# Modulation sums of a transformer kernel: VectorE turns the rows in 32 by 32 blocks, four products with stacked identities add the quarters

## The chip, the cores and the metric

The kernel runs on one core of a Trainium2 chip. A core has TensorE (PE, with its weight loads as PEld), VectorE (DVE), ScalarE (ACT), GpSimd (POOL) and SyncE (SP, which issues transfers), on-chip memory SBUF with 128 partitions, and PSUM, eight banks that TensorE writes. The metric is the device time of one execution in microseconds (us).

## The reference, cut to what matters

The program runs two blocks on 256 tokens of width 1024. The first has two layers of a gated feed-forward part, a mixing part (Fourier mixing, dilated attention, differential attention, gates) and a second feed-forward part. The second block has one layer of attention and a mixture of 32 experts, modulated by a vector `c`:

```python
c_act = jax.nn.silu(c)                                   # (1, 1024)
mod = (c_act @ w_ada[l] + b_ada[l])[:, None, :]          # 6 x 1024 values
shift1, scale1, gate1, shift2, scale2, gate2 = jnp.split(mod, 6, axis=-1)
h = _rmsnorm(x, norm1_w[l]) * (1.0 + scale1) + shift1
```

The modulation is a product of one row with a matrix of 1024 x 6144. It depends on no other result, so the kernel computes it earlier, inside the first block.

## The kernel before, in words

Activations lie transposed in SBUF: 128 channels of a group on the partitions, 256 tokens along. Weights come as a stream of tiles of 1.5 MB into a ring of four, mostly three units of 128x1024 to a tile. ScalarE rounds each unit to its high part (`round_unit`, L467), VectorE takes the rest as its low part (`low_unit`, L864), and TensorE multiplies with three products for each block (L1413, L1416, L1417, and L1444 to L1448 in `project_tok`). Four buffers of each part let the engines run ahead of TensorE.

The two layers of the first block are one loop (`Fori(0, LAYERS)`). Each engine has its own program with its own fixed order, tied to the others by semaphores. In a layer the steps are: feed-forward, projections, attention in 12 steps u (four dilated, eight differential), the V20 projection (eight units, c = 0 to 7), the Fourier mixing, gates and branches, output, feed-forward.

The modulation tiles lie in the stream: seven (`ADA_TILES`) in each layer, two behind the loop. `ada_tile` (L1481) multiplies one of them on TensorE in attention step u, from u = 6 on. Its weight operand `cpad` is 32 columns wide, of which only the first holds silu(c). Each of the four groups of 32 PSUM partitions gets two of the eight channel groups, so the sum of a modulation value lies in four quarters, in partitions 0, 32, 64 and 96 of bank 5, in 384 columns; the other rows are zero. ScalarE copies these 128x384 values to SBUF (`ada_sb`, L608; L656 behind the loop), as its last work of the step, and raises `ada_row`, for which TensorE waits before the next tile. `ada_sums` (L1490) then makes columns of the rows: for each tile and each 128 of its 384 values one product, whose weight is the 128x128 block of `ada_sb` and whose moving operand is one column of ones:

```python
for i in range(n):
    pe.wait_ge(ada_row, rows + i + 1)
    for j in range(ADA_COLS):
        at = 384 + i * ADA_COLS + j
        mm = mm_(ps[:, bank, at:at + 1], ada_sb[i][:, j * P:(j + 1) * P], ones[:, 0:1], start=True, stop=True)
```

These are 21 products in each layer, behind unit c = 2 of V20 (L1602), and 6 behind the loop, behind the first unit of the second block (L1687). The products are in fp32, and each is two records in the trace. VectorE copies the resulting columns to `mod` at c = 3 (L1039).

In an attention step VectorE scales the logits and adds the bias (`scores`, L1003, then the maximum at L1008 or L1010), and then divides the exponentials of the step before (`probs`, L1017 to L1022). TensorE does the logits of u (L1550), the transposes of u - 2 (L1559), the values of u - 3 (L1568, L1579) and then the modulation tile (L1487). ScalarE does the exponentials (L580, L584), copies the transposes (L590), the outputs (L605) and the modulation rows (L608).

Of the kernel before, what the change touches and what calls it, by code (L numbers as in the profile page):

```python
# [11 lines left out]
ALU = mybir.AluOpType  # L12
ACT = mybir.ActivationFunctionType
# [96 lines left out]
def build(nc, stream, experts, x_in, konst_in, cpad_in, layer_in, lam_in, cols_in, relb_in, onehot_in, konst1_in,  # L110
          konst2_in, bias_rows, out):
    with ExitStack() as ctx:
# [32 lines left out]
        lamv = rest("lamv", 18432, LAYERS, 4 * DH)  # L145
# [20 lines left out]
        ada_sb = [rest(f"ada_sb{i}", 16384 + 384 * i if i < 5 else 3328 + 384 * (i - 5), 384) for i in range(ADA_TILES)]  # L166
# [93 lines left out]
        rel_landed, konst1_landed, konst2_landed = sem("rel_landed"), sem("konst1_landed"), sem("konst2_landed")  # L260
        cpad_ready, cols_landed = sem("cpad_ready"), sem("cols_landed")
# [195 lines left out]
        def _(a):  # L457
# [83 lines left out]
            with a.Fori(0, LAYERS) as l:  # L541
# [51 lines left out]
                for u in range(UNITS + 3):  # L593
# [12 lines left out]
                    if 6 <= u < 6 + ADA_TILES:  # L606
                        a.wait_ge(ada_used, l * ADA_TILES + (u - 5))
                        nc.scalar.activation(ada_sb[u - 6][:, :], ps[:, 5, 0:384], ACT.Copy).then_inc(ada_row, 1)  # L608
# [45 lines left out]
            for i in range(2):  # L654
                a.wait_ge(ada_used, L * ADA_TILES + i + 1)
                nc.scalar.activation(ada_sb[i][:, :], ps[:, (3, 0)[i], 0:384], ACT.Copy).then_inc(ada_row, 1)  # L656
# [199 lines left out]
        def _(v):  # L856
# [85 lines left out]

            for i in range(OUTS):
                v.wait_ge(xt_ready, i + 1)
                nc.vector.tensor_copy(x[:, 2 * i:2 * i + 2, :], ps[:, 4 + i, :].rearrange("p (a b) -> p a b", b=TOK)).then_inc(x_ready, 1)
            v.wait_ge(par_landed, 16)
# [5 lines left out]
            with v.Fori(0, LAYERS) as l:  # L952
# [73 lines left out]
                for u in range(UNITS + 1):  # L1026
                    if u < UNITS:
                        scores(u)
                    if 1 <= u <= UNITS:
                        probs(u - 1)  # L1030
                    if u == 7:
                        v.wait_ge(ob_hi, l + 1)
                        nc.vector.tensor_tensor(obs[:, 1, :], ps[:, 6, 0:TOK], obs[:, 0, :].bitcast(F32), ALU.subtract).then_inc(ob_taken, 1)
                low_unit(l, V20 + 2)
# [56 lines left out]
            v.wait_ge(cols_landed, 16)  # L1091
            recip_std(Q)
# [308 lines left out]
        def _(pe):  # L1401
# [88 lines left out]
            def ada_sums(n, bank, rows):  # L1490

                for i in range(n):
                    pe.wait_ge(ada_row, rows + i + 1)
                    for j in range(ADA_COLS):
                        at = 384 + i * ADA_COLS + j
# [698 lines left out]
```

## Time and profile before

| | |
|---|---|
| median of 3 runs | 2830.42 us (2827.72 to 2830.92) |
| profiled execution | 2826.78 us, span 2825.0 us |
| granted TensorE clock, mean | 0.966 of 2.4 GHz |
| PE busy | 2669.5 us (94%), 19672 matmul records |
| DVE busy | 1435.2 us (51%) |
| ACT busy | 942.2 us (33%) |
| DMA, mean over the span | 251 GB/s |

Rows of the profile give start and duration in microseconds, the engine, the line of the kernel and the operation with the names and shapes it writes and reads. `128*32 128x384` on a matmul is a weight of 128 rows and 32 columns and 384 moving columns. A bracket `[1.43 <-PE ps L1550]` says how long the engine sat idle before and what ended it. Repeated rows are merged as `xN`, with the time from the first to the end of the last.

### The profile page before, as it was taken

The page shows a single profiled execution, that of the slowest core. Times are in us where ns is not written, and L with a number is a line of the kernel's source. Part 1 is how long each engine was busy: PE and PEld are TensorE (multiplying, and loading weights), DVE is VectorE, ACT ScalarE, POOL GpSimd, SP SyncE. Part 2 cuts the span into 40 slices and gives each one's busy share as a digit, 9 for nine tenths or more (in the row PEclk, how much of TensorE's full clock was granted, in tenths as well). Part 3 has the DMA queues.
Part 4 walks back from the last instruction along what each step waited for, and adds up shares of the span by engine and source line. Part 5 has one row for each costly group of instructions (what it writes and reads, how often), then busy time and mean ns, then how long its engine had stood idle before and what let it go on. Part 6 is the DMA issues. An engine that isn't in the chain of part 4 may idle for free.

```text
span 2825.0 us, 49664 instructions
## 1 busy us (share of the span) xinstructions
PE 2669.5 (94%) x19672; PEld 2150.2 (76%) x19673; DVE 1435.2 (51%) x2586; ACT 942.2 (33%) x1471; POOL 30.5 (1%) x21
## 2 busy tenths in 40 slices
PE   7999999999899999999979879799999999999996
PEld 6999689999899868999968869755555555555553
DVE  5665556666566555666656775423333333333333
ACT  4444444443444445444434534211111111111111
POOL 0000000000000000000000210000000000000000
PEclk8999999999999989999989989889999999999997
DMA  8644535455355453445433324469999999999994
GB/s 257 235 178 158 223 113 184 161 187 183 140 187 186 158 238 131 179 157 179 182 152 135 112 90 148 158 268 430 429 431 429 431 430 430 430 430 430 430 430 201
DMA packets 70406, 709.15 MB, mean 251 GB/s; under 512 B 10983, under 2 KB 11239, under 8 KB 13303
## 3 DMA queue, kind: packets, MB, share of 16 engines
q1 hardware_dynamic: 65144, 699.30, 61.8%
q0 software_dynamic: 5152, 8.31, 1.4%
q8 instruction: 77, 1.26, 0.2%
q14 instruction: 33, 0.27, 0.0%
HBM read 703.89 MB, written 3.67 MB: 250 GB/s over the span
## 4 chain that ended last, share of the span: by engine, by line
PE 70%; DMA 19%; DVE 7%; ACT 2%; issue 2%; SPq 0%; DVEq 0%; ACTq 0%
DMA slot<-in_experts 19%; PE ps L1413 15%; PE ps L1416 15%; PE ps L1417 15%; PE ps L1898 5%; PE ps L1881 4%; PE ps L1923 3%; PE ps L1936 1%; PE ps L1408 1%; PE ps L1444 1%; PE ps L1447 1%; PE ps L1448 1%; DVE u_lo L864 1%; PE ps L1487 1%; PE ps L1550 1%
## 5 line engine op out<-in xcount | busy, mean ns | idle before, releaser
L864 DVE TENSOR_TENSOR u_lo<-ring,u_hi 128x1024 fp32r<-128x1024 f32 x500 | 615.8, 1237 | 498.9 <-ACT u_hi L467 495.2
L467 ACT ACTIVATE u_hi<-ring 128x1024 fp32r<-128x1024 f32 x498 | 523.7, 1057 | 705.2 <-PE ps L1413 633.1
L1413 PE MATMUL ps<-hs,u_hi 128*128 128x256 f32 x2408 | 692.3, 287 | 24.4 <-DVE hs L883 22.9
L1416 PE MATMUL ps<-hs,u_hi 128*128 128x256 f32 x2408 | 685.7, 285 | 0.0
L1417 PE MATMUL ps<-hs,u_lo 128*128 128x256 f32 x2408 | 685.6, 285 | 0.0
L1413 PEld LDWEIGHTS ps<-hs,u_hi 128*128 128x128 f32 x2408 | 466.6, 194 | 36.2 <-DVE hs L883 22.8
L1898 PE MATMUL ps<-slot,xg 128*64 128x256 f32 x4096 | 472.0, 381 | 10.1 <-DMA slot<-in_experts 9.7
L1416 PEld LDWEIGHTS ps<-hs,u_hi 128*128 128x128 f32 x2408 | 466.7, 194 | 0.5
L1417 PEld LDWEIGHTS ps<-hs,u_lo 128*128 128x128 f32 x2408 | 466.6, 194 | 0.0
L1898 PEld LDWEIGHTS ps<-slot,xg 128*64 128x64 f32 x4096 | 290.9, 137 | 222.9 <-issue 74.1
L1923 PE MATMUL ps<-slot,eact 128*64 128x512 f32 x1024 | 249.2, 607 | 5.6 <-DMA slot<-in_experts 5.1
L1344 DVE TENSOR_SCALAR lin<-ps,konst 128x64 f32<-128x64 f32 x256 | 71.3, 278 | 333.2 <-PE ps L1908 333.2
L1335 DVE SCALAR_TENSOR_TENSOR y_tok<-ps,wt,y_tok 128x512 f32<-128x512 f32 x128 | 90.2, 747 | 248.8 <-PE ps L1936 248.8
L1413 PE MATMUL ps<-acts,u_hi 128*128 128x256 f32 x704 | 199.7, 284 | 3.4 <-DVE acts L911 3.4
L803 ACT ACTIVATE hid_tok<-ps 128x256 f32<-128x256 f32 x128 | 49.0, 383 | 457.5 <-PE ps L1898 457.5
L1416 PE MATMUL ps<-acts,u_hi 128*128 128x256 f32 x704 | 199.2, 283 | 0.0
L1417 PE MATMUL ps<-acts,u_lo 128*128 128x256 f32 x704 | 199.2, 283 | 0.0
L1881 PEld LDWEIGHTS ps<-place,h_tok 128*128 128x128 f32 x1024 | 120.0, 196 | 27.4 <-issue 23.1
L1923 PEld LDWEIGHTS ps<-slot,eact 128*64 128x64 f32 x1024 | 62.1, 136 | 101.5 <-issue 97.3
L1413 PEld LDWEIGHTS ps<-acts,u_hi 128*128 128x128 f32 x704 | 135.1, 192 | 4.2 <-issue 4.2
L1416 PEld LDWEIGHTS ps<-acts,u_hi 128*128 128x128 f32 x704 | 135.1, 192 | 0.0
L1417 PEld LDWEIGHTS ps<-acts,u_lo 128*128 128x128 f32 x704 | 135.1, 192 | 0.0
(313 smaller groups left out, 3077.8 us busy)
## 6 DMA issues: line engine op xcount, KB each, us to landing
slot<-in_experts SPq DMA_DIRECT2D x256, 1536.0 KB, 20.4
ring<-in_stream SPq DMA_DIRECT2D x184, 1536.0 KB, 6.4
slot<-in_experts SPq DMA_DIRECT2D x4, 1024.0 KB, 4.8
bias<-bias_rows POOLq DMA_DIRECT2D x2, 1280.0 KB, 11.3
konst<-in_konst POOLq DMA_DIRECT2D x1, 2272.0 KB, 14.7
bias_rows<-vecs POOLq DMA_DIRECT2D x3, 512.0 KB, 14.1
x_tok<-in_x SPq DMA_DIRECT2D x1, 1024.0 KB, 5.3
bias_rows<-vecs POOLq DMA_DIRECT2D x1, 1024.0 KB, 70.6
```

Source lines behind the costliest of these rows:

```text
L467: nc.scalar.activation(u_hi[buffer_of(l, k)][:, :], raw_unit(l, k), ACT.Copy).then_inc(unit_hi, 1)
L803: nc.scalar.activation(hid_tok[:, j % 2, :], ps[:, j % 2, 0:2 * P], ACT.Copy).then_inc(htok_copied, 1)
L864: nc.vector.tensor_tensor(u_lo[b][:, :], raw_unit(l, kk), u_hi[b][:, :].bitcast(F32), ALU.subtract).then_inc(unit_lo, 1)
L1335: nc.vector.scalar_tensor_tensor(out=ys, in0=ps[:, 6 + half, :], scalar=wt[:, t, bass.ds(e, 1)], in1=ys, op0=ALU.mult, op1=ALU.add).then_i ...
L1344: nc.vector.tensor_scalar(lin[:, j % 2, h, :], ps[:, 3, h * P + CAP:h * P + 2 * CAP], konst2[:, bass.ds(e * 16 + (K2_BEXP + DC + c), 1)], ...
L1408: mm = mm_(ps[:, SSUM, 0:TOK], ones, sq[:, c, :], start=c == 0, stop=c == DC - 1)
L1413: mm = mm_(dst, hi, x_hi, start=first, stop=False, skip_group_check=True)
L1416: mm_(dst, hi, x_lo, start=False, stop=False, skip_group_check=True)
L1417: return mm_(dst, lo, x_hi, start=False, stop=last, skip_group_check=True)
L1881: mm = mm_(ps[:, 2, c * CAP:(c + 1) * CAP], h_tok[:, t, c * P:(c + 1) * P], place[:, t, 0:CAP], start=t == 0, stop=t == TT - 1)
L1898: mm = mm_(ps[h * CAP:(h + 1) * CAP, j % 2, 0:2 * P], xg[:, b, k * PAIRS + c, :], slot(2 * j + k)[:, at:at + 2 * P], start=k == 0 and c == ...
L1923: mm = mm_(ps[h * CAP:(h + 1) * CAP, 4, :], eact[:, j % 2, k, :], slot(sl)[:, at:at + 512], start=j == 0 and k == 0, stop=j == PAIRS - 1 a ...
```

## The change

VectorE takes over from ScalarE. Instead of a copy it does a `transpose` of the 128x384 PSUM values into `adaT`, which turns each block of 32x32 by itself: the value in partition 32q, column 32b + i comes to partition 32q + i, column 32b. `turn_ada` waits for the tile (`ada_used`) and stands before `scores(u)` for u = 7 to 11, before the last `probs` at u = 12, and once more behind the steps; the two behind the loop stand before the first `recip_std`. The weight of the sums is now `quarters`, four stacked 32x32 identities, made once at the start of the program by a `tensor_reduce` over the identity. Four products, one for each group r of 32 output partitions, take every 128th column of `adaT` from 32r on and so add the four quarters of all n tiles at once (21 moving columns in a layer, 6 behind the loop). `lamv` moves to another place in SBUF, `adaT` lies at 16384, where most of `ada_sb` was.

```diff
-        lamv = rest("lamv", 18432, LAYERS, 4 * DH)
+        lamv = rest("lamv", 3328, LAYERS, 4 * DH)
...
-        ada_sb = [rest(f"ada_sb{i}", 16384 + 384 * i if i < 5 else 3328 + 384 * (i - 5), 384) for i in range(ADA_TILES)]
+        adaT = rest("adaT", 16384, ADA_TILES * 384)
+        quarters = rest("quarters", 19072, 32)
...
-                    if 6 <= u < 6 + ADA_TILES:
-                        a.wait_ge(ada_used, l * ADA_TILES + (u - 5))
-                        nc.scalar.activation(ada_sb[u - 6][:, :], ps[:, 5, 0:384], ACT.Copy).then_inc(ada_row, 1)
...
-            for i in range(2):
-                a.wait_ge(ada_used, L * ADA_TILES + i + 1)
-                nc.scalar.activation(ada_sb[i][:, :], ps[:, (3, 0)[i], 0:384], ACT.Copy).then_inc(ada_row, 1)
...
+            def turn_ada(l, i, bank):
+
+                v.wait_ge(ada_used, l * ADA_TILES + i + 1)
+                nc.vector.transpose(adaT[:, i * 384:(i + 1) * 384], ps[:, bank, 0:384]).then_inc(ada_row, 1)
...
+            v.wait_ge(konst_landed, 16)
+            nc.vector.tensor_reduce(quarters[:, :], ident.rearrange("p (a b) -> p b a", b=32), AX.X, ALU.add).then_inc(quarters_ready, 1)
...
                 for u in range(UNITS + 1):
+                    if 7 <= u <= UNITS:
+                        turn_ada(l, u - 7, 5)
                     if u < UNITS:
                         scores(u)
...
+                turn_ada(l, ADA_TILES - 1, 5)
                 low_unit(l, V20 + 2)
...
+            for i in range(2):
+                turn_ada(L, i, (3, 0)[i])
             recip_std(Q)
...
-                for i in range(n):
-                    pe.wait_ge(ada_row, rows + i + 1)
-                    for j in range(ADA_COLS):
-                        at = 384 + i * ADA_COLS + j
-                        mm = mm_(ps[:, bank, at:at + 1], ada_sb[i][:, j * P:(j + 1) * P], ones[:, 0:1], start=True, stop=True)
+                pe.wait_ge(ada_row, rows + n)
+                for r in range(4):
+                    mm = mm_(ps[32 * r:32 * r + 32, bank, 384:384 + n * ADA_COLS], quarters[:, :], adaT[:, 32 * r:n * 384:P], start=True, stop=True)
                 mm.then_inc(ada_cols, 1)
...
             pe.wait_ge(vec_taken, 4)
+            pe.wait_ge(quarters_ready, 1)
```

## Rows read from the trace of the kernel before

**Rows 1.** The page, part 4: the chain that ended last, by engine.

```profile
PE 70%; DMA 19%; DVE 7%; ACT 2%; issue 2%; SPq 0%; DVEq 0%; ACTq 0%
```

**Rows 2.** The chain of waits, layer 1: start us, us, what.

```profile
343.91 5.52 PE ps L1496 x42
349.44 0.64 PE ps L1444
...
354.12 0.30 PE ps L1444
```

**Rows 3.** The chain of waits, layer 2.

```profile
1045.89 4.58 PE ps L1496 x42
1050.47 0.51 PE ps L1444
...
1054.59 0.23 PE ps L1444
...
1057.02 0.23 PE ps L1444
```

**Rows 4.** By stretches: us, PE, PEld, DVE, ACT, POOL busy, clock, DMA share, GB/s.

```profile
343.90:349.40 5.50, 5.50 (x44) 5.50 (x42) 0.16 (x1) 0.00 (x0) 0.00 (x0) 0.81 0.89 371
349.40:354.10 4.70, 4.70 (x14) 4.12 (x14) 1.32 (x2) 1.06 (x1) 0.00 (x0) 0.50 0.04 14
354.10:361.70 7.60, 7.60 (x39) 6.77 (x38) 3.68 (x3) 3.19 (x3) 0.00 (x0) 1.00 0.50 171
...
1050.40:1054.10 3.70, 3.70 (x12) 3.12 (x12) 1.31 (x2) 1.06 (x1) 0.00 (x0) 0.54 1.04 442
```

**Rows 5.** The timeline of TensorE behind the loop: start us, us, what.

```profile
1450.82 1.39 PE L1496 MATMUL ps<-konst,ada_sb 128*128 128x1 f32 x12
1452.07 0.47 PE L1444 MATMUL ps<-u_hi,hs 128*128 128x512 f32 x1
```

**Rows 6.** The timeline of TensorE's weight loads at a modulation tile.

```profile
1420.52 0.13 PEld L1487 LDWEIGHTS ps<-ring,cpad 128*32 128x32 f32 x4 [0.19 <-issue]
```

**Rows 7.** The timeline of VectorE (and one weight load) in the attention steps, layer 1.

```profile
320.30 0.42 DVE L1033 TENSOR_TENSOR obs<-ps,obs 128x256 fp32r<-128x256 f32 x1
320.81 0.69 DVE L1003 SCALAR_TENSOR_TENSOR S<-ps,bias 128x512 f32<-128x512 f32 x1
...
322.77 0.48 DVE L1022 SCALAR_TENSOR_TENSOR S<-S,small 128x256 f32<-128x256 f32 x1
...
329.76 0.69 DVE L1003 SCALAR_TENSOR_TENSOR S<-ps,bias 128x512 f32<-128x512 f32 x1 [0.59 <-PE ps L1550]
...
332.33 0.17 DVE L1020 RECIPROCAL small<-small 128x2 f32<-128x2 f32 x1
...
332.99 0.48 DVE L1022 SCALAR_TENSOR_TENSOR S<-S,small 128x256 f32<-128x256 f32 x1
...
334.92 0.20 PEld L1559 LDWEIGHTS ps<-konst,S 128*128 128x128 f32 x2 [0.62 <-issue]
...
339.09 1.23 DVE L864 TENSOR_TENSOR u_lo<-ring,u_hi 128x1024 fp32r<-128x1024 f32 x1 [5.61 <-ACT u_hi L467]
```

**Rows 8.** Single lines of VectorE: durations in ns (min/median/max); one timeline row.

```profile
L945 DVE COPY x<-ps x4: 680/692/692, 7.7 to 10.0; 128x512 f32<-128x512 f32 x4
...
303.30 0.96 DVE L1003 SCALAR_TENSOR_TENSOR S<-ps,bias 128x768 f32<-128x768 f32 x1 [1.60 <-PE ps L1550]
...
L1018 DVE TENSOR_SCALAR S<-S,small x8: 619/620/622, 298.5 to 1011.2; 128x768 f32<-128x768 f32 x8
...
L1042 DVE RECIPROCAL std<-std x2: 6553/6553/6553, 367.4 to 1067.8; 128x1024 f32<-128x1024 f32 x2
```

**Rows 9.** The timelines of ScalarE and VectorE in V20, layer 2.

```profile
1047.35 1.06 ACT L467 ACTIVATE u_hi<-ring 128x1024 fp32r<-128x1024 f32 x1 [4.14 <-DMA ring<-in_stream]
...
1048.43 1.22 DVE L864 TENSOR_TENSOR u_lo<-ring,u_hi 128x1024 fp32r<-128x1024 f32 x1 [3.60 <-ACT u_hi L467]
```

**Rows 10.** By stretches, in the dilated steps of layer 1.

```profile
297.00:301.00 4.00, 2.00 (x9) 1.40 (x9) 3.90 (x7) 1.64 (x4) 0.00 (x0) 0.82 0.00 0
301.00:305.00 4.00, 4.00 (x14) 2.74 (x13) 2.33 (x4) 1.72 (x3) 0.00 (x0) 0.50 0.00 0
```

More of the change, by code:

```diff
@@ L260, in build @@
         rel_landed, konst1_landed, konst2_landed = sem("rel_landed"), sem("konst1_landed"), sem("konst2_landed")
+        quarters_ready = sem("quarters_ready")
         cpad_ready, cols_landed = sem("cpad_ready"), sem("cols_landed")
```

## The prediction

> **What bounds the kernel now.** I read the page first, then the chain of waits around the lines that the change touches, then the timeline of each engine there, then the clock by stretches. TensorE carries 70% of the chain that ended last, VectorE 7% and ScalarE 2% [rows 1]. So what leaves TensorE's queue should shorten the program unless another engine takes its place.
>
> In the chain of layer 1 the reader sees the sums at L1496: 42 records, 5.52 us in one piece, with no other engine in between [rows 2]. Behind them the next unit starts at 349.44 and the one after it at 354.12: 4.68 us for a unit of products that takes 2.43 us undisturbed (1054.59 to 1057.02) [rows 3]. The stretches explain it: the granted clock is 0.81 during the sums, 0.50 (1.2 GHz of 2.4) for the 4.7 us behind them, and 1.00 again after that [rows 4]. The engine had work all the time, but work of one column each, and the clock fell. Layer 2 shows the same: 4.58 us of sums, then a unit that takes 4.12 us from 1050.47 to 1054.59 [rows 3], at a clock of 0.54 [rows 4]. The third place, behind the loop, has only 12 records: 1.25 us from the first to the product behind them, which is not a slow one [rows 5].
>
> **The change part by part.**
>
> *Sums removed.* Layer 1: 5.52 us of records, and 4.68 - 2.43 = 2.25 us lost by the clock, with 0.07 in the product at 354.12 (0.30 for 0.23): 2.3. Layer 2: 4.58, and 4.12 - 2.43 = 1.7. Third place: 1.25. Together 5.52 + 2.3 + 4.58 + 1.7 + 1.25 = 15.4 us, all in TensorE's queue and on the chain.
>
> *Four products in their place.* Each fp32 product is two records (21 products are 42), so there are 8 records, three times. No row shows a 32-column weight with 21 columns moving. Nearest are those of the modulation tiles: 32-column weights, four column groups side by side, four loads in 0.13 us with 0.19 us of issue before them, so 0.32 us for four [rows 6]; 8 records make 0.64. From below: loads alone, 0.26 us. From above: the pace of the old records, 4.58/42 = 0.109, makes 0.87, with 0.3 us more for the change of weight shape before and after: 1.2. I take 0.7 us, as the modulation rows are the nearest: 2.1 us for three. That a stretch of 8 records lets the clock stay up is read from the third place, where 12 did [rows 5].
>
> Balance of TensorE: 15.4 - 2.1 = 13.3 us.
>
> *Turning in place of ScalarE's copies.* ScalarE loses 16 copies of 0.48 us. In every step it waits for VectorE's maxima, so this is worth nothing. VectorE gains 16 turns of 128x384 from PSUM. The trace has no such operation. A copy of 128x512 from PSUM takes 0.69 us, and the scores (L1003) grow from 0.69 at 512 columns to 0.96 at 768, 1.05 ns a column [rows 7, 8], so a copy of 384 columns would take 0.69 - 0.13 = 0.56 us. From below: the 768 columns of L1018 in 0.62 us are 0.81 ns a column all told, 0.31 us. From above: VectorE's slowest row, the reciprocal, 6.4 ns a column [rows 8], 2.46 us. I take 0.56 us, for it reads the same memory with one input and no arithmetic.
>
> The Trainium skill speaks against this value. "VectorE: DVE Perf Modes", section "The three transpose paths", gives 311 ns for a 128x128 block turn in bf16, and three such are an estimate of 0.93 us; the microarchitecture page ("Vector Engine (DVE) Microarchitecture Reference", section 3.8) has the turn sustain one element per cycle and lane, which is near the 0.56 us. No row here decides between them; by 0.93 us the sum would be 3 us smaller.
>
> *What a turn costs in the attention steps.* There is one step per modulation tile, and VectorE is nearly as full as TensorE. From the start of the scores (L1003) to the end of the last probabilities (L1022) are 323.25 - 320.81 = 2.44 us; then it waits some 0.6 us for the next logits [rows 7]. The turn stands before the scores. The first, at u = 7, fits into VectorE's wait for that step's logits and costs nothing. The second follows L1033, which ends at 320.72, where there is no idle time: with 0.56 and 0.02 of handing over, the scores start at 321.32, not at 320.81. From there a step of VectorE takes 2.44 + 0.58 = 3.02 us against the 2.98 of now (320.81 to 329.76 in three), so three steps later the last scores start at 321.32 + 9.06 = 330.38 instead of 329.76: 0.62 us late. Queued behind the waiting turn are the scores and probabilities of the step; for the probabilities wait TensorE's transposes. The turn at u = 12 stands before the last probabilities: 330.38 + 2.44 + 0.58 + 1.14 (L1020 to L1022) = 334.54, some 0.5 us to hand over, and TensorE comes to the last transposes only at 334.92 [rows 7] + 0.62, behind its last tile, so nothing is added. Cost: 0.6 us a layer, 1.2 in all. The seventh turn lies in the 5.61 us idle before 339.09 [rows 7], the two behind the loop where VectorE waits for the root.
>
> *The wait on the turns moved.* TensorE's wait before a tile is met when the turn ends, about when the scores start; its tile comes behind transposes and values of the same step. The sums' wait is long met by c = 2. The reduction that makes the stacked identities and TensorE's wait for it stand where VectorE idles for the first unit: nothing. So is the place of lamv.
>
> *What comes late next.* With the sums gone TensorE needs later units sooner. In layer 1 none waits for a transfer. In layer 2 ScalarE waited 4.14 us for the tile of unit 93 (c = 5), and VectorE made its low part by 1049.65 [rows 9]. TensorE would come to c = 5 at 1045.89 + 0.6 + 0.7 + 2 x 2.43 = 1052.05, and the low part, 0.6 later as well, is there at 1050.25: 1.8 us to spare. Later stages, the expert stage with its transfers too, follow from what comes before and move along.
>
> *Sum.* 13.3 - 1.2 = 12.1 us. The profiled execution took 2826.78 us (span 2825.0, 1.8 around it); so it would be 2814.7. The median of the three runs is 3.6 above that execution, so the forecast is 2830.42 - 12.1 = 2818.3 us.
>
> **The rivals.**
>
> *The turn goes over its columns twice* (fill the blocks, then empty them): 0.56 + 384 x 1.05 = 0.96 us. By the same steps: 320.74 + 0.98, three steps of 3.42, the last scores at 331.98, 2.2 us late. Sum 13.3 - 4.4 = 8.9: 2821.5 us. For it speaks that nothing here shows the operation; against it the even price per column of the plain VectorE rows. Three times the 311 ns of the Trainium skill's "VectorE: DVE Perf Modes" would come to nearly this. Chance 0.15.
>
> *The clock falls all the same behind the shorter sums.* Then 2.3 + 1.7 = 4.0 us stay: 2822.3 us. Against it the third place. Chance 0.08.
>
> *Layer 2 waits for its tile instead.* Once the tile lands over 1.8 us later, each microsecond is lost, up to the layer's 5.6 us: at worst 2823.9. The transfer engines are full there (1.04) [rows 4]. Chance 0.04.
>
> *Slower: VectorE becomes the bound of the attention steps.* Were the turn as slow per column as the reciprocal (2.46 us), the second scores would start at 323.22, each step take 4.92, the last scores 337.98; with the turn at u = 12 and the probabilities, then some 0.5 to hand over, TensorE has them at 344.5 instead of 334.92: 9.6 us a layer, 19.2 for 13.3 gained, 2836.3 us. It decides from about 1.85 us a turn, where the cost is 6.6 us a layer. There the clock could also go: after a stretch with TensorE busy 2.00 of 4 us it was 0.50 [rows 10], and a step of 4.92 us would have it busy some 2.9. Chance 0.04.
>
> The change does what it says: the rows read are the same sums, so a rival of "no effect" has no mechanism.
>
> **How the numbers follow.** Forecast 0.69, with its own range of 2815 to 2821.5 (sums of 0.26 to 1.2 us: 1.3 less to 1.5 more in all; a turn of 0.31 to 0.75: 1.2 less to 1.6 more). Under 0.2% (5.7 us) a measurement of this kernel cannot be told from no change: 2824.8 to 2836.1. The range runs from 2813.5, where both low bounds meet and the runs fall below their median as they do now (by up to 2.7 us), to 2825, where the first two rivals meet. Faster: 0.69 + 0.13 + 0.07 + 0.02 = 0.91, of which I leave 0.02 for what no row shows: 0.89. Same: the ends of the rivals together, 0.07. Slower: 0.04.
>
> **What would show it.** L1496 should have 8 records a place in under 1.2 us; the unit behind it 2.43 us at a clock of 1.00; the turns 0.5 to 0.6 us each, before L1003; the last L1003 of a layer about 0.6 us later against the first; ScalarE without L608; no wait of TensorE at c = 5 of layer 2. The forecast is wrong if a turn takes over 0.8 us, if the clock is 0.50 behind the sums, or if a new wait for a transfer stands in the chain.

## The result and the profile after

The changed kernel took 2810.41 us, median of four runs (2808.21 to 2813.28), beside 2830.48 us for the kernel before in the same session: ratio 0.9931, 95% interval [0.9917, 0.9946], 20.1 us less. In two later sessions the medians of the changed kernel were 2809.5 and 2811.45 us, both 17.4 us below those of the kernel before; the ratios, 0.9944 [0.9930, 0.9958] and 0.9943 [0.9929, 0.9956], make it 15.8 and 16.1 us. (The ratio is not exactly that of the medians: in the first session it makes 19.5 of the 20.1 us.) The forecast was 2818.3 us, 12.1 us less, with a range that ended at 2813.5. The direction was right, the gain was larger than forecast, and the time lies below the range. The profiled executions stand 13.5 us apart (2826.78 and 2813.28).

The page of the changed kernel, its span, part 1 and part 4 (the last line answers to [rows 1]):

```profile
span 2811.5 us, 49508 instructions
...
PE 2659.6 (95%) x19600; PEld 2141.0 (76%) x19601; DVE 1443.0 (51%) x2603; ACT 935.7 (33%) x1455; POOL 30.6 (1%) x21
...
PE 69%; DMA 20%; DVE 7%; ACT 2%; issue 2%; SPq 0%; DVEq 0%; ACTq 0%
```

These are the shares of the kernel before to within a point: TensorE still carries the chain.

The chain of waits behind the attention steps of layer 1, and the place of the sums in layer 2 (start us, us, what). It answers to [rows 2, 3]:

```profile
344.82 0.21 PE ps L1502 x8
345.03 0.43 PE ps L1452
345.46 0.23 PE ps L1455
...
347.68 0.23 PE ps L1452
...
1040.07 0.21 PE ps L1502 x8
1040.28 0.43 PE ps L1452
```

The reader sees 8 records in 0.21 us where 42 took 5.52, one product behind them of 0.43 instead of 0.23, and then a unit that is over by 347.68: 2.65 us from its start, 0.22 more than the 2.43 of an undisturbed unit.

The same by stretches (us, PE, PEld, DVE, ACT, POOL busy, clock, DMA share, GB/s); it answers to [rows 4]:

```profile
344.80:345.40 0.60, 0.60 (x11) 0.51 (x11) 0.17 (x1) 0.00 (x0) 0.00 (x0) 1.00 0.86 369
345.40:352.40 7.00, 7.00 (x37) 6.25 (x36) 3.47 (x4) 3.18 (x3) 0.00 (x0) 1.00 0.75 277
1040.50:1050.00 9.50, 9.50 (x48) 8.45 (x48) 5.65 (x6) 5.19 (x5) 0.00 (x0) 1.00 1.00 428
```

The granted clock stays at 1.00 (2.4 GHz) behind both places, where it was 0.50 and 0.54.

The turn, in the summary of its line (ns min/median/max), and VectorE's timeline in the attention steps of layer 1. It answers to [rows 7]:

```profile
L942 DVE STREAM_TRANSPOSE adaT<-ps x16: 572/582/583, 318.1 to 1410.6; 128x384 f32<-128x384 f32 x16
...
321.47 0.57 DVE L942 STREAM_TRANSPOSE adaT<-ps 128x384 f32<-128x384 f32 x1
321.96 0.65 DVE L1006 SCALAR_TENSOR_TENSOR S<-ps,bias 128x512 f32<-128x512 f32 x1
...
324.29 0.57 DVE L942 STREAM_TRANSPOSE adaT<-ps 128x384 f32<-128x384 f32 x1
324.79 0.65 DVE L1006 SCALAR_TENSOR_TENSOR S<-ps,bias 128x512 f32<-128x512 f32 x1
...
330.71 0.69 DVE L1006 SCALAR_TENSOR_TENSOR S<-ps,bias 128x512 f32<-128x512 f32 x1
```

A turn is recorded with 0.58 us, but the scores start 0.49 to 0.50 us after the turn does: records of VectorE that follow each other overlap by some 0.08 us. A step is (330.71 - 321.96)/3 = 2.92 us. It was 2.98. Measured from the same point of each trace, the start of the low part before the attention steps, the first scores shown start 0.3 us later than in the kernel before and the last 0.1 us later, where the forecast had 0.5 and 0.6.

ScalarE's wait for the tile of layer 2 is there still, 3.81 us for 4.14, and nothing of the chain hangs on it (answers to [rows 9]):

```profile
1040.93 2.01 ACT L469 ACTIVATE u_hi<-ring 128x1024 fp32r<-128x1024 f32 x2 [3.81 <-DMA ring<-in_stream]
```

The third place, timeline of TensorE (answers to [rows 5]): 0.18 us from the first of the eight to the product behind them, for 1.25.

```profile
1438.47 0.25 PE L1502 MATMUL ps<-adaT,quarters 128*32 128x6 f32 x8
1438.65 0.50 PE L1452 MATMUL ps<-u_hi,hs 128*128 128x512 f32 x1
```

To compare kernels whose spans differ elsewhere, I measured each trace between the same low-part records of VectorE (L864 before, L860 after; 503 of them in every kernel, numbered in order of time). The change touches four stretches: 78 to 90 (projection's end and the attention steps of layer 1), 90 to 98 (V20 with the sums, layer 1), 290 to 306 (both, layer 2) and 417 to 421 (the third place). "Rest" is the span less these four; its instructions are the same in all kernels, but for the small reduction at the start that makes the identities. Times are us, each of one profiled execution:

```
kernel             78-90  90-98  290-306  417-421  touched    span    rest
before             82.00  23.79   119.17    13.56    238.5  2825.0  2586.4
before, again      81.99  23.75   119.17    13.53    238.4  2826.5  2588.1
changed            82.08  16.35   113.50    12.48    224.4  2811.5  2587.1
changed, again     83.52  16.36   112.10    12.41    224.4  2805.8  2581.4
changed, third     83.48  16.36   112.09    12.36    224.3  2806.2  2581.9
e1_spare_sums      83.57  22.62   119.96    13.94    240.1  2830.6  2590.5
e2_spare_spread    82.08  21.01   116.76    14.98    234.8  2821.8  2586.9
e3_dve_copies      82.07  23.77   119.58    13.42    238.8  2823.8  2584.9
e4_early_tiles     83.78  17.12   114.62    13.41    228.9  2809.7  2580.8
e5_double_turns    85.29  16.35   115.29    13.59    230.5  2816.1  2585.6
e6_narrow_many     83.49  18.31   115.35    13.61    230.8  2820.3  2589.5
e7_spare_wide      82.13  24.19   121.22    13.89    241.4  2828.5  2587.0
e8_turn_later      87.24  16.35   117.25    12.47    233.3  2821.0  2587.7
e9_full_filler     83.52  23.20   118.94    12.39    238.1  2819.1  2581.0
```

Where the change acts it brings 238.5 - 224.4 = 14.1 us, in each pair of traces. That is the number to hold against the steps of the forecast. What the timed runs show beyond it, 1.7 us (by a later ratio) to 6.0 us (by the first medians), has to lie outside, in what the last column counts. That column differs by 9.7 us between kernels with the same instructions there, and the first pair of traces shows no gain in it at all (2586.4 and 2587.1).

The touched columns, too, hold something that is not the change. The first and the third contain the dilated steps [rows 10], before any turn. There the clock is down for a shorter or a longer time, in traces whose instructions are the same up to that point. Stretches from the low part before the attention steps of layer 1 to the second one after it (before, changed, changed again):

```profile
285.22:339.09 53.87, 49.28 (x332) 32.86 (x331) 32.38 (x63) 28.37 (x74) 0.00 (x0) 0.94 0.49 198
...
286.05:339.99 53.94, 49.32 (x332) 32.97 (x331) 35.72 (x69) 25.60 (x67) 0.00 (x0) 0.94 0.49 198
...
284.20:339.59 55.39, 52.16 (x331) 34.61 (x331) 35.74 (x70) 25.62 (x67) 0.00 (x0) 0.88 0.47 192
```

At a mean clock of 0.94 the stretch takes 53.9 us, at 0.88 it takes 55.4. In layer 2 it is the same 1.4 us: 53.8 at 0.87, 52.4 at 0.93 or 0.94. In the three traces of the changed kernel the two layers happen to cancel, which is why the sum repeats so well. In the last touched column the clock counts as well: 0.94 to 0.96 in most traces, but 0.87 in e2 and 0.85 to 0.87 in e4, e5 and e6. Where a reading below compares "at like clock", it takes for each column a trace with the same clock there.

### The profile page after: what moved, and what is told of

Same layout as the page of the kernel before. It is cut to its first block, busy times and chain, and to the rows that moved or that the text cites. A ratio compares the mean times of both kernels' runs of the same rounds, so it can differ in the third digit from the quotient of the medians.

```text
span 2811.5 us, 49508 instructions
## 1 busy us (share of the span) xinstructions
PE 2659.6 (95%) x19600; PEld 2141.0 (76%) x19601; DVE 1443.0 (51%) x2603; ACT 935.7 (33%) x1455; POOL 30.6 (1%) x21
## 4 chain that ended last, share of the span: by engine, by line
PE 69%; DMA 20%; DVE 7%; ACT 2%; issue 2%; SPq 0%; DVEq 0%; ACTq 0%
DMA slot<-in_experts 19%; PE ps L1421 15%; PE ps L1424 15%; PE ps L1425 15%; PE ps L1905 5%; PE ps L1888 4%; PE ps L1930 3%; PE ps L1943 1%; PE ps L1416 1%; PE ps L1452 1%; PE ps L1455 1%; PE ps L1456 1%; DVE u_lo L860 1%; ACT u_hi L469 1%; DVE acc L1190 1%
## 5 line engine op out<-in xcount | busy, mean ns | idle before, releaser
L860 DVE TENSOR_TENSOR u_lo<-ring,u_hi 128x1024 fp32r<-128x1024 f32 x500 | 615.8, 1237 | 481.1 <-ACT u_hi L469 477.4
## 6 DMA issues: line engine op xcount, KB each, us to landing
slot<-in_experts SPq DMA_DIRECT2D x256, 1536.0 KB, 20.5
bias_rows<-vecs POOLq DMA_DIRECT2D x3, 512.0 KB, 14.1
```

Of the source, the lines that this page charges most:

```text
L860: nc.vector.tensor_tensor(u_lo[b][:, :], raw_unit(l, kk), u_hi[b][:, :].bitcast(F32), ALU.subtract).then_inc(unit_lo, 1)
```

## The experiments

The kernels of one session share runs of the kernel before, whose median was 2826.89, 2827.28, 2828.88 and 2829.31 us in the four sessions. "Local" below is the column "touched" above.

**The pair once more: after_again, after_third, before_again.** The two kernels, with no edit.

> The changed kernel, unchanged. Two profiled executions stood 13.5 us apart in span, two medians 20.1 us. Theory 1 (the granted clock falls at other places and more or less often from execution to execution, and the profiled execution of the kernel before was a short one, that of the changed one a long one): the ratio stays between 0.992 and 0.995, and the new profile has a span some us off 2811.5 with the same durations of the instructions that the change touches. Theory 2 (chance of one session): the ratio comes nearer 0.9957, which is the forecast.

> The changed kernel once more, for a third trace and more timed runs. By the traces so far the change itself is worth 14.1 us in the stages that it touches, the same in both; what lies above that comes from stages whose instructions are the same in both kernels and whose clock falls at other places from execution to execution. The ratio should lie between 0.993 and 0.996, and the stages outside the touched ones should again differ from the other two traces by 1 to 3 us.

> The kernel before, unchanged, for a second trace of it. Theory 1: the stretches at clock 0.50 behind the sums have another length than in the first trace (4.7 and 3.7 us there), and those in stages that the change doesn't touch differ too; the records of the sums keep their 0.109 us where the clock is 1.00.

Measured: 2809.5 (ratio 0.9944) and 2811.45 us (0.9943) for the changed kernel, 2828.34 us in one run for the one before. The local gain repeats within 0.1 us. The rest does not: 2587.1, 2581.4 and 2581.9 us in three traces of one kernel. The third trace was expected 1 to 3 us from both others there; it lies 5.2 and 0.5 us from them. The second trace of before was expected to have the low clock behind the sums for another length; it has the same, 0.51 for 4.8 us, and its touched columns repeat within 0.04 us:

```profile
345.25 5.33 PE ps L1496 x42
350.57 0.64 PE ps L1444
```

```profile
345.50:351.00 5.50, 5.50 (x40) 5.41 (x40) 0.00 (x0) 0.00 (x0) 0.00 (x0) 0.81 0.85 344
351.00:355.80 4.80, 4.80 (x14) 4.20 (x13) 1.32 (x2) 1.13 (x2) 0.00 (x0) 0.51 0.04 14
```

**e1_spare_sums: the changed kernel with the old records put back.** Behind the four new products stand the 42 (or 12) old ones, on the turned rows, into columns that nothing reads.

```diff
+            def spare_sums(n, bank, i0=0):
+                for i in range(i0, i0 + n):
+                    for j in range(ADA_COLS):
+                        at = 416 + i * ADA_COLS + j
+                        mm = mm_(ps[:, bank, at:at + 1], adaT[:, i * 384 + j * P:i * 384 + (j + 1) * P], ones[:, 0:1], start=True, stop=True)
+                return mm
...
+                mm = spare_sums(n, bank)
                 mm.then_inc(ada_cols, 1)
```

> The changed kernel with the 48 products of one column put back behind the four new ones, as idle work that nobody reads (21 in a layer in one place, 6 behind the loop). It measures the whole term of the sums, clock included. By the terms of the prediction it costs 5.5 + 2.3 + 4.6 + 1.7 + 1.25 = 15.4 us: about 2825.8. If the clock loss behind the sums is larger in most executions than in the profiled one (theory 1), it costs 18 to 21 us and comes near 2830. If the clock plays no part it costs the records alone, 96 x 0.109 = 10.5 us: 2821.

Measured: 2830.02 us, ratio to before 1.0011 [1.0002, 1.0020]. The whole gain is gone. Local it is 240.1 - 224.4 = 15.7 us more than the changed kernel, also at like clock in the dilated steps (83.57 and 119.96 beside 83.52 and 112.10). By the medians of the session it is 20.5 us more, so what the timed runs show beyond the touched stretches has gone as well. TensorE's timeline:

```profile
345.87 4.94 PE L1503 MATMUL ps<-konst,adaT 128*128 128x1 f32 x42
...
351.25 0.63 PE L1455 MATMUL ps<-u_lo,hs 128*128 128x512 f32 x1
...
354.92 0.39 PE L1455 MATMUL ps<-u_lo,hs 128*128 128x512 f32 x1
```

A product of 512 columns is recorded with 0.63 us for 3 us behind the sums, and with 0.39 later. So what the change gains where it acts comes from the records and from what they do to the clock, and nothing that can be seen here from ScalarE's copies or from the new place of the waits.

**e2_spare_spread: the same records in pieces.** Each tile's six records stand behind another unit of V20 (and the third place's behind two), so that the work is the same and the unbroken stretch is gone. The four new products move behind them, to c = 6, and VectorE's copy of the columns to c = 7.

```diff
-                    if c == 2:
+                    if c == 0:
+                        pe.wait_ge(ada_row, (l + 1) * ADA_TILES)
+                    if c < 7:
+                        spare_sums(1, 5, c)
+                    if c == 6:
                         ada_sums(ADA_TILES, 5, l * ADA_TILES)
```

> The same 48 idle products, but three behind each V20 unit c = 0 to 6 (and three behind each of the first two units behind the loop), the four new products behind c = 6 and VectorE's copy of their columns at c = 7. The same records, never more than 0.65 us of them in one piece. If the clock falls because of one long stretch of one-column work, this costs 10.5 us (2821) and its profile has a clock of 1.00 in all of V20. If the kind or the number of records costs more than their pace, it costs as much as the kernel with all in one place.

Measured: 2823.49 us, ratio 0.9984 [0.9975, 0.9993]; 6.5 us faster than e1, in the same session, and 5.3 us less local. Timeline of TensorE, and the clock over V20 of layer 1 by stretch:

```profile
339.00 0.72 PE L1503 MATMUL ps<-konst,adaT 128*128 128x1 f32 x6
```

```profile
338.00:365.00 27.00, 27.00 (x150) 22.97 (x149) 11.21 (x11) 14.25 (x17) 0.00 (x0) 1.00 0.67 259
```

The pieces cost their own time and the clock is 1.00 throughout, and so it is in V20 of layer 2. By the plain sums of the table this splits the removed 15.7 us into 10.4 for the records (234.8 - 224.4) and 5.3 for the clock. At like clock it is 4.66 in layer 1 (21.01 - 16.35), 4.66 in layer 2 (116.76 - 112.10) and 1.5 at the third place (13.94 - 12.4 of e1, since e2's own 14.98 stands at a clock of 0.87): 10.8 us for the records, where the forecast had 5.52 + 4.58 + 1.25 = 11.35, and 4.9 for the clock, where it had 4.0.

**e3_dve_copies: the kernel before, with the copies on VectorE.** Sums as before; ScalarE's 16 copies move to the place of the turns.

```diff
-                        a.wait_ge(ada_used, l * ADA_TILES + (u - 5))
-                        nc.scalar.activation(ada_sb[u - 6][:, :], ps[:, 5, 0:384], ACT.Copy).then_inc(ada_row, 1)
...
+                v.wait_ge(ada_used, l * ADA_TILES + i + 1)
+                nc.vector.tensor_copy(ada_sb[i][:, :], ps[:, bank, 0:384]).then_inc(ada_row, 1)
```

> The kernel before with VectorE instead of ScalarE copying the modulation rows, at the places where the change turns them; the old sums stay. It measures the load on VectorE in the attention steps alone. By the prediction 1.2 us slower than before. By the trace of the changed kernel, where instructions of VectorE overlap by 0.08 us at each end and the steps grew by some 0.1 us in all: no difference that can be measured (under 0.5 us).

Measured: 2826.73 us, ratio 0.9997 [0.9988, 1.0006]; local 238.8 for 238.5. VectorE's timeline shows that a plain copy costs what a turn does:

```profile
323.31 0.55 DVE L940 COPY ada_sb<-ps 128x384 f32<-128x384 f32 x1
323.78 0.68 DVE L1002 SCALAR_TENSOR_TENSOR S<-ps,bias 128x512 f32<-128x512 f32 x1
```

It starts 0.47 us before the scores, a turn 0.49 to 0.50. The 0.3 us of local difference are a net: in layer 1, at like clock, the copies cost 0.07 us (82.07 for 82.00); in layer 2 the dilated steps were 1.4 us shorter, at the higher clock, and V20 some 1.9 us longer, at a mean clock of 0.93 for 0.97. So VectorE takes this load at some 0.1 us a layer, as far as one trace shows. The forecast had 0.6.

**e5_double_turns: how near VectorE's bound is.** The first six turns of each layer are done twice, once into a spare tile, in the attention steps alone.

```diff
+                if i < ADA_TILES - 1 and bank == 5:
+                    nc.vector.transpose(spare[:, :], ps[:, bank, 0:384])
```

> The changed kernel with a second, idle turn before each of the first six in a layer. It tests where the slower rival begins. VectorE's steps in the changed kernel's trace run back to back, with 0.49 to 0.50 us from the start of a turn to the next instruction: if they are at the bound, five of the six extra turns cost 0.5 us each, 5 us in all (2815). If there is still slack in the steps, it costs under 2 us.

Measured: 2817.24 us, ratio 0.9960 [0.9945, 0.9975], against 0.9944 of the changed kernel some 4.5 us more; the two were timed in different sessions and the intervals overlap, so the trace has to carry the reading. Local it is 6.1 us more. At like clock it is 1.8 us in each layer (85.29 for 83.52, and 115.29 for the 113.50 of the first trace), 3.6 in both; the rest is the clock, in the dilated steps of layer 2 and at the third place, where nothing was edited (13.59 at 0.85). VectorE's timeline:

```profile
322.45 0.65 DVE L1009 SCALAR_TENSOR_TENSOR S<-ps,bias 128x512 f32<-128x512 f32 x1
...
324.78 0.57 DVE L944 STREAM_TRANSPOSE spare<-ps 128x384 f32<-128x384 f32 x1
325.28 0.54 DVE L945 STREAM_TRANSPOSE adaT<-ps 128x384 f32<-128x384 f32 x1
325.74 0.65 DVE L1009 SCALAR_TENSOR_TENSOR S<-ps,bias 128x512 f32<-128x512 f32 x1
```

The step is now 325.74 - 322.45 = 3.29 us, 0.37 more than with one turn for 0.47 us of added work: so some 0.1 us was to spare. Five such steps in a layer are 1.85 us, the 1.8 of the columns. One turn a step was nearly free and a second one costs four fifths of its length: with a second turn VectorE bounds these steps, as the fourth rival had it, from far less than the 1.85 us at which its loss outweighs the gain.

**e8_turn_later: the turn behind the scores.** If VectorE's load is what counts, a turn that does not hold up the scores should cost no more.

```diff
-                    if 7 <= u <= UNITS:
-                        turn_ada(l, u - 7, 5)
                     if u < UNITS:
                         scores(u)
+                    if 7 <= u <= UNITS:
+                        turn_ada(l, u - 7, 5)
```

> The changed kernel with each turn behind the scores of its step and before the probabilities, instead of before the scores. VectorE's work is the same; the maxima reach ScalarE 0.5 us sooner, the probabilities come at the same time. In the changed kernel's chain the turn stands between the probabilities and the scores at u = 8 and u = 11. If that place matters: 0.5 to 1 us a layer less, 2808 to 2810. If VectorE's total decides: no difference to 2810.

Measured: 2822.86 us, ratio 0.9978 [0.9967, 0.9988]: 11.4 us slower than the changed kernel in the same session, 8.9 local by the plain sums and 10.3 at like clock (87.24 for 82.08, 117.25 for 112.10). A clear miss. The timeline of all engines in one step:

```profile
322.01 0.69 DVE L1006 SCALAR_TENSOR_TENSOR S<-ps,bias 128x512 f32<-128x512 f32 x1 [0.88 <-PE ps L1557]
...
323.33 0.57 DVE L942 STREAM_TRANSPOSE adaT<-ps 128x384 f32<-128x384 f32 x1
...
324.04 1.50 PE L1495 MATMUL ps<-ring,cpad 128*32 128x384 f32 x16 [1.27 <-DVE adaT L942]
...
325.47 0.70 PE L1557 MATMUL ps<-qk 64*128 64x256 f32 x4
...
326.22 0.69 DVE L1006 SCALAR_TENSOR_TENSOR S<-ps,bias 128x512 f32<-128x512 f32 x1 [1.29 <-PE ps L1557]
```

Tile, turn, logits and scores form a ring. All tiles go through one PSUM bank; the next tile waits for the turn of the last (1.27 us), the logits (L1557) are queued behind the tile on TensorE, and the scores wait for the logits (1.29 us). The step grows to 326.22 - 322.01 = 4.21 us. The forecast's sentence on the moved wait, that it is met before TensorE comes to the next tile, holds for the place that the change chose, and by less than the 1.3 us by which this edit delays the turn (scores and maxima, 322.01 to 323.33).

**e4_early_tiles: the tiles in steps that wait anyway.** The modulation tiles begin with the second step instead of the seventh, five of the seven in bank 7, so that TensorE has them while it waits in the dilated steps [rows 10]. Before bank 7 gets its next use TensorE waits for the fifth turn, and the turn behind the steps falls away.

```diff
-                    if 7 <= u <= UNITS:
-                        turn_ada(l, u - 7, 5)
+                    if 2 <= u < 2 + ADA_TILES:
+                        turn_ada(l, u - 2, 7 if u < 7 else 5)
...
-                    if 6 <= u < 6 + ADA_TILES:
-                        if u == 6:
+                    if 1 <= u < 1 + ADA_TILES:
+                        if u == 1:
```

> The changed kernel with the seven modulation tiles of a layer multiplied in attention steps u = 1 to 7 instead of 6 to 12 (the first five into bank 7, which is free then), and turned one step later. In the changed kernel's trace TensorE and VectorE are both full in the steps with tiles, while in the dilated steps before them TensorE idles and its clock falls to 0.50. If the steps with tiles are bound by TensorE as much as by VectorE, five tiles of 1.43 us leave full steps and fill idle ones: 3 to 5 us a layer, about 2802. If VectorE alone bounds them, moving TensorE's work gains nothing, and the turns added to the dilated steps (VectorE busy 3.9 of 4 us there) cost about 0.5 us each: 2812 to 2814.

Measured: 2811.58 us, ratio 0.9946 [0.9933, 0.9960], the same as the changed kernel's 0.9944. No gain. By stretches:

```profile
301.00:305.00 4.00, 3.83 (x33) 2.37 (x22) 3.37 (x6) 1.72 (x3) 0.00 (x0) 1.00 0.87 356
320.00:336.00 16.00, 11.45 (x75) 7.43 (x76) 13.90 (x31) 8.11 (x29) 0.00 (x0) 0.89 0.66 270
336.00:352.00 16.00, 16.00 (x82) 13.99 (x82) 7.26 (x7) 8.52 (x10) 0.00 (x0) 0.89 0.27 99
```

The dilated steps gained what was hoped for: the clock is 1.00 in the stretch that had 0.50 [rows 10]. But the later steps, now without tiles, have TensorE busy 11.45 of 16 us, and the clock is 0.89 there and in the V20 units behind. The loss moved; locally it is even 4.5 us more, 1.0 of it at the third place, where the clock was 0.87 for 0.95.

**e6_narrow_many, e7_spare_wide: what it is in the sums that lowers the clock.** e6 repeats the four new products 20 times a layer (160 records of 32-column weights); e7 is e1 with 21 columns moving in each old record, not one. The second diff is against e1, with the operand shortened to `[...]`; its columns also go to three places in turn.

```diff
-                for r in range(4):
+                for r in list(range(4)) * (20 if n == ADA_TILES else 1):
```

```diff
-                        mm = mm_(ps[:, bank, at:at + 1], adaT[...], ones[:, 0:1], start=True, stop=True)
+                        mm = mm_(ps[:, bank, at:at + 21], adaT[...], ones[:, 0:21], start=True, stop=True)
```

> The changed kernel with the four products in each layer done 20 times (160 records in place of 8). One group of 8 records takes 0.21 us in its trace, so 19 more are 4.0 us a layer, about the length of the old sums. If a long stretch of products with few columns makes the clock fall, whatever their weights, it costs 8 us and 4 to 6.5 us of clock behind: 2822 to 2825, with a stretch at 0.50 behind the products. If it was the 128-column weights with one column moving, it costs 8 us alone: 2818.

> The changed kernel with the same 48 idle products as in the run that put the old sums back, but each with 21 columns of ones moving instead of one. The weights and the records are the same, and the records' pace is that of the weight loads (0.109 us), so their own cost is the same 10.5 to 11 us. If the clock fell because almost no columns moved, it stays up now: about 2821, 6 to 9 us below the 2830.0 of that run. If 128-column fp32 weights loaded without pause are what lowers it, or the length of the stretch, it falls again: 2828 to 2830.

Measured: e6 2818.42 us, ratio 0.9966 [0.9955, 0.9977], local 6.4 more than the changed kernel; e7 2830.13 us, 1.0003 [0.9994, 1.0012], local 17.0 more. TensorE's timeline, e6 first:

```profile
345.76 2.25 PE L1502 MATMUL ps<-adaT,quarters 128*32 128x21 f32 x160
...
348.28 0.40 PE L1455 MATMUL ps<-u_lo,hs 128*128 128x512 f32 x1
```

```profile
344.83 5.89 PE L1503 MATMUL ps<-konst,adaT 128*128 128x21 f32 x42
...
351.13 0.63 PE L1455 MATMUL ps<-u_lo,hs 128*128 128x512 f32 x1
```

Behind e7's records products are slow for over 4 us, so the single moving column is not the cause: 42 loads of a whole 128-column weight, each with little to multiply, lower the clock with 21 columns too. The records of e7 took 5.89 us and those of e1 4.94, but that is the clock again and not the columns. By stretches, of these records alone (us, PE, PEld, clock, DMA share, GB/s):

```profile
344.83:348.33 3.50, 3.50 (x32) 3.50 (x32) 1.00 0.98 411
348.43:350.55 2.12, 2.12 (x12) 2.12 (x11) 0.50 0.51 214
```

At a clock of 1.00 e7's records start 0.112 us apart, as e1's do with one column; at 0.50 they start 0.213 us apart (both from the starts of the single records). In e1 the clock fell only at the end of the 42, in e7 some ten records earlier.

e6 does not answer what it was meant to. Its 160 records ran in 2.2 us, not the 4.0 that I had expected, so it shows that 2.2 us of narrow products leave the clock up (0.40 for the product behind them), and not what a stretch as long as the old one would do. The time came out at the 2818 of the second branch, by luck: of the local 6.4 us only 3.8 are the added records at like clock (1.96 in layer 1, 1.85 in layer 2), and the others are the clock in the dilated steps and at the third place. Whether it is the width of the weights or the length of the stretch that counts is therefore not shown; with e2, only that 128-column weights in pieces of six records do not lower it.

**e9_full_filler: is it the place in time that helps the later stages?** Eight products of 512 columns at full clock stand behind the four, 7.06 us a layer, which puts the later stages back to within some 1 us of where they were (the 298th low part, in V20 of layer 2, starts at 1041.5 us, before at 1042.5) without lowering the clock.

```diff
+                if n == ADA_TILES:
+                    for r in range(8):
+                        mm = mm_(ps[:, 4, :], ones, adaT[:, 0:512], start=True, stop=True)
```

> The changed kernel with eight idle products of 512 columns (fp32, 16 records of 0.43 us) behind the four new ones in each layer: 6.9 us of full TensorE work where the old sums took 6 to 8 us with their clock loss, so all later stages start about where they did in the kernel before. If the timed gain above the 14.1 us of the touched stages comes from where the later stages fall in time, this kernel comes back to the kernel before, within 1 us of it. If it doesn't, the kernel is 13.8 us above the changed one: 2824 to 2824.5, some 3 us faster than before. Stretches behind the filler have a clock of 1.00 either way.

Measured: 2822.45 us, ratio 0.9977 [0.9968, 0.9986]. Chain of waits:

```profile
343.94 0.21 PE ps L1502 x8
344.15 7.06 PE ps L1505 x16
351.21 0.23 PE ps L1452
```

Local it is 238.1, only 0.4 us less than before; yet it is 6.5 us faster than before in the timed runs, and its rest is 2581.0 us. So the time at which the later stages begin does not, by itself, make them slow or fast.

## Why the forecast was right in direction and too small

**The sums, 15.4 us: right; their two parts mis-sized the opposite way.** e1 puts them back and costs 15.7 us local. At like clock the records alone are 10.8 us, not 11.35, and the clock is 4.9, not 4.0. The forecast had booked the 5.52 us of layer 1 as records, although the same 42 took 4.58 in layer 2. The stretches of these records alone in the kernel before (us, PE, PEld, clock, DMA share, GB/s) show why:

```profile
343.91:347.21 3.30, 3.30 (x32) 3.30 (x31) 1.00 1.01 421
347.41:349.41 2.00, 2.00 (x10) 1.94 (x10) 0.50 0.66 283
```

The clock fell before the records were through; the last ones start 0.213 us apart, the others 0.112. The mean of 0.81 in [rows 4] is these two levels. The 0.94 us between 5.52 and 4.58 are the clock's, and with them moved the forecast's parts would have been 10.4 and 4.9. The sum is not touched by that.

**The new products, 0.7 us a place: too dear.** In the layers, 0.21 us of chain and 0.20 in the product behind them make 0.41. At the third place it is 0.18 and 0.03 (0.50 for 0.47). In all three 1.0 for 2.1. The nearest row, the loads of the modulation tiles [rows 6], was the wrong neighbour: its 0.32 us for four hold 0.19 us of issue, which the eight records, all within 0.21 us, do not show.

**The turn, 0.56 us: right; its cost in the steps, 1.2 us: mis-sized.** The turn took 0.58. Of the two statements weighed, the one element per cycle of the Trainium skill's "Vector Engine (DVE) Microarchitecture Reference", section 3.8, fits, and the estimate of 0.93 us from the Trainium skill's "VectorE: DVE Perf Modes", "The three transpose paths", does not; the first rival falls with it. But the forecast added durations (2.44 + 0.58 = 3.02), while records overlap by 0.08 us: a turn puts 0.49 to 0.50 into a step, and the step became 2.92, shorter than the 2.98 of before. At like clock the stretch of the attention steps in layer 1 grew by 0.07 us, with the turns as with the copies of e3; in layer 2 it is 53.78 for 53.88 and 53.66. So it is some 0.1 us a layer or less, for 0.6: 1.0 us back. Once VectorE is the bound, though, its load is paid (e5).

**Together, where the change acts.** In the two layers the forecast was 12.1 - (1.25 - 0.7) = 11.55 us; with 0.6 back from the products and 1.0 from VectorE that is 13.15, and 13.0 were measured (224.96 less 211.93, the sums of the first three columns). At the third place it was 0.55, 1.04 with the measured products, and the pair shows 1.1. e4, e5 and e6, with the changed kernel's instructions there, have 13.4 to 13.6 us like the kernel before, but at a clock of 0.85 to 0.87; at 0.94 to 0.96 the traces with the 12 records have 13.4 to 13.9 us and those without 12.4 to 12.5. So this microsecond is the change's.

**Clock behind the short sums, and the tile of layer 2: right.** The clock is 1.00 behind both places, and TensorE meets no new wait for a transfer there, so the second and third rival fall.

**VectorE as the bound: right in mechanism, not reached.** e5 shows that one turn fills the steps to within 0.1 us and a second is paid. e8 shows a way to be slower that no rival named: not VectorE's load but the ring through the one PSUM bank, 5.2 us a layer.

**From one pair of traces to the medians: the step that failed.** The forecast put the untouched stages at nothing ("Later stages, the expert stage with its transfers too, follow from what comes before and move along"), took 12.1 us off the median and let the runs fall at most 2.7 below it. (Its low bounds make 2815.8, and 2813.1 with the 2.7; it wrote 2815 and 2813.5, which changes nothing here.) Of the 8.0 us that it missed in the first session, 2.0 lie where the change acts and are the two mis-sized terms above. With 14.1 us alone the median would have been 2816.4 us, inside the range. The other 6.0 us (3.3 by the medians of the later sessions) lie in stages with the same instructions.

These stages take 2580.8 to 2590.5 us over 14 traces. The first pair does not show their gain, because it ran the other way round: the profiled execution of the kernel before was 3.6 us below its median, that of the changed kernel 2.9 above. The two later traces of the changed kernel do: 2581.4 and 2581.9, against 2586.4 and 2588.1 before. Three stages make most of it, counted in low parts. In the first two a shorter time goes with a higher mean clock (in brackets) for the same instructions; in the third the mean clock does not separate the values:

- 400 to 417: 77.2 us in both traces of before and in e1 (mean clock 0.90), 76.9 in the first trace of the changed kernel and 77.0 in e8 (0.90), 75.9 in its other two traces and in e2, e3, e5, e6, e7 and e9 (0.92 to 0.94), 74.2 in e4 (0.95).
- 421 to 445: 86.3 to 86.5 us in both of before, e1, e3 and e7 and 86.0 in e5 and e6 (0.96), 85.2 to 85.3 in the three of the changed kernel and in e2, e4, e8 and e9 (0.98).
- 445 to 466: 123.4 us in the first trace of the changed kernel (0.92), 120.5 to 120.6 in its other two and in e9 (0.93 to 0.94), 121.7 to 121.9 in all others (0.92 to 0.93).

For the later traces of the changed kernel against before these are 1.3 + 1.2 + 1.3 = 3.8 us, of the size of the 3.3 that the later medians show beyond 14.1. What decides where the clock is down in these stages is open. It is not the place in time alone (e9), and what the timed runs show beyond the touched stretches went away when the old records were put back (e1: 20.5 us timed for 15.7 local). The first session's 20.1 us is larger than the 17.4 of both later ones, though its interval (15.3 to 23.5 us) holds them; the median of before was also 1.2 to 3.6 us higher there than later. A range drawn for this kernel has to hold some 5 us for these stages, on either side.

## What to carry to other kernels

Count what an unbroken run of weight loads with little to multiply does to the clock behind it, beside its own time: here a third of the gain (4.9 of 15.7 us) was not in the removed records at full clock. For the load on an engine near its bound take the distance from start to start, not the recorded duration, and ask which ring the moved instruction stands in: the same turn costs next to nothing ahead of the scores and 10 us more behind them. Read the clock within a stretch and not only behind it: where the same records take 5.52 us in one place and 4.58 in another, the difference is not theirs. And a forecast of 0.5% for a long kernel needs the spread of the stages that it does not touch, which one trace cannot give.

## What the runs showed of the hardware that was not expected

- Products with 32-column weights in four column groups, 21 columns moving, run at 2.25/160 = 0.014 us a record, against 0.112 us for a 128-column weight with the same 21 columns at full clock (e7), eight times as much. The Trainium skill's "TensorE: Matmul & The Clock Gate", section "Wait — 56ns, not 53.3ns?", says that start-to-start never falls below about 25 ns however few columns move; the records here, in four column groups, start closer than that.
- 21 moving columns instead of one cost a record of a 128-column weight nothing: 0.112 us from start to start with either, at a clock of 1.00, and 0.213 at 0.50. They saved the clock nothing either.
- A turn of 128x384 in 32 by 32 blocks out of PSUM costs what a copy of the same shape does: 0.57 and 0.55 us.
- Work moved into a stretch where the clock was low lifted it there (0.50 to 1.00), and the clock was lower where the work had been (0.89, e4): no net gain.
- The attention steps of layer 1, the dilated ones among them, take 53.9 or 55.4 us in traces of one and the same kernel, at a mean clock of 0.94 or 0.88: an uncertainty of 1.4 us in any comparison of single traces that contains them.
